# Latent query and key norms computed in the Fourier stage, and one Fourier stage for tokens and context

## The reference

```python
def rms_norm(x, g):
    xf = x.astype(jnp.float32)
    y = xf * lax.rsqrt(jnp.mean(jnp.square(xf), axis=-1, keepdims=True) + NORM_EPS) * g
    return y.astype(x.dtype)

def fourier_mix(z):
    zg = z.reshape(b, n, FNET_GROUPS, FNET_GROUP_DIM).astype(jnp.float32)   # 4 groups of 128
    return jnp.fft.fft2(zg, axes=(1, 3), norm='ortho').real                 # tokens and channels

def mixer(h, hc, lp, rope, n_rows, need_ctx):       # need_ctx: in the first layer only
    f, nq, nk, nv, cq, ckv, kr, g = jnp.split(h @ lp['w_in'], IN_OFFSETS, axis=-1)
    y_f = fourier_mix(f)
    y_na = neighbourhood_attention(...)
    mla_k, mla_v = mla_keys_values(ckv, kr, ...)    # rms_norm(ckv, g_kv) @ w_uk, @ w_uv; rope on kr
    mla_q = mla_queries(cq, ...)                    # rms_norm(cq, g_q) @ w_uq, @ w_qr; rope
    y_mla = blocked_attend(mla_q, ...)
    out = merge_branches([y_f, y_na, y_mla], g, lp['w_branch'], lp['w_out'])
    if need_ctx: the same three branches for the context
```

## Time and profile before

| | |
|---|---|
| time, median of 3 runs | 3474.93 us (3470.12, 3474.93, 3482.54) |
| the profiled execution: its time | 3475.75 us |
| its span (first to last instruction) | 3473.8 us |
| TensorE busy | 3015.1 us (87%) |
| VectorE busy | 1763.6 us (51%) |
| ScalarE busy | 1197.6 us (34%) |
| GpSimd busy | 448.9 us (13%) |
| mean granted clock of TensorE | 0.921 of 2.4 GHz |

### The profile page before, as it was taken

The page is one execution under the profiler, slowest core; times in us unless marked ns, Lnnn a source line. Parts: engine busy times, 40 slices in busy tenths (PEclk is TensorE's granted clock), DMA queues, the critical chain, the costliest instruction groups (busy, mean ns, idle before and its releaser), DMA issues. The chain is left out here.

```text
span 3473.8 us, 37971 instructions
## 1 busy us (share of the span) xinstructions
PE 3015.1 (87%) x15109; PEld 2392.6 (69%) x15109; DVE 1763.6 (51%) x2555; ACT 1197.6 (34%) x1746; POOL 448.9 (13%) x419
## 2 busy tenths in 40 slices
PE   5788879799987999999698798987999968875995
PEld 3677646688875888888487455775878745553774
DVE  4564666222236554553512763345555453644886
ACT  4322645212114211221323543223322233533884
POOL 3410310000011000001320200001000013212232
PEclk8799989999997999999899899998999988986997
DMA  5663010222212443431340102322655415514972
GB/s 158 114 161 97 1 22 1 73 55 55 55 43 67 120 122 96 118 108 51 52 94 26 22 0 73 91 73 61 182 164 173 134 28 70 162 49 150 339 269 73
DMA packets 398087, 330.33 MB, mean 95 GB/s; under 512 B 38059, under 2 KB 340697, under 8 KB 397785
## 3 DMA queue, kind: packets, MB, share of 16 engines
q1 hardware_dynamic: 384664, 304.79, 30.9%
q0 software_dynamic: 13248, 23.13, 3.4%
HBM read 332.09 MB, written 30.33 MB: 104 GB/s over the span
## 5 line engine op out<-in xcount | busy, mean ns | idle before, releaser
L1043 PE MATMUL ps<-ahi,w_hi 128*128 128x512 f32 (+1 forms) x2384 | 865.0, 363 | 164.8 <-DVE alo L710 91.5
L1045 PE MATMUL ps<-alo,w_hi 128*128 128x512 f32 (+1 forms) x2384 | 854.1, 358 | 0.0
L1044 PE MATMUL ps<-ahi,w_lo 128*128 128x512 f32 (+1 forms) x2384 | 853.5, 358 | 0.0
L1043 PEld LDWEIGHTS ps<-ahi,w_hi 128*128 128x128 f32 x2384 | 459.0, 193 | 250.6 <-issue 67.9
L1065 DVE TENSOR_TENSOR w_lo<-w_raw,w_hi 128x1024 fp32r<-128x1024 f32 (+2 forms) x248 | 359.7, 1452 | 422.9 <-ACT w_hi L1055 422.3
L1045 PEld LDWEIGHTS ps<-alo,w_hi 128*128 128x128 f32 x2384 | 458.7, 192 | 67.6
L1044 PEld LDWEIGHTS ps<-ahi,w_lo 128*128 128x128 f32 x2384 | 459.6, 193 | 63.7
L1055 ACT CAST w_hi<-w_raw 128x1024 fp32r<-128x1024 f32 (+2 forms) x248 | 289.8, 1170 | 425.8 <-PE ps L1045 349.8
L877 DVE SCALAR_TENSOR_TENSOR vec_acc<-vec_w,csilu,vec_acc 128x512 f32<-128x512 f32 x364 | 260.8, 762 | 19.9 <-DMA vec_w<-in_w_mod 15.1
L1043 PE MATMUL ps<-hhi,w_hi 128*128 128x512 f32 (+1 forms) x528 | 190.5, 361 | 10.1 <-DVE hlo L1174 10.1
L1141 POOL TENSOR_TENSOR xsum<-x 128x768 f32<-128x768 f32 (+1 forms) x4 | 7.2, 1800 | 1480.0 <-DVE x L1126 1480.0
(11 more groups left out here) (497 smaller groups left out, 5195.6 us busy)
## 6 DMA issues: line engine op xcount, KB each, us to landing
vec_w<-in_w_mod SPq DMA_DIRECT2D x128, 512.0 KB, 3.9
w_raw<-in_w_in SPq DMA_DIRECT2D x104, 512.0 KB, 4.2
e_raw<-in_w_gate SPq DMA_DIRECT2D x46, 512.0 KB
e_raw<-in_w_up SPq DMA_DIRECT2D x46, 512.0 KB
e_raw<-in_w_down SPq DMA_DIRECT2D x46, 512.0 KB
w_raw<-in_w_ffn_gate SPq DMA_DIRECT2D x44, 512.0 KB, 3.9
w_raw<-in_w_ffn_up SPq DMA_DIRECT2D x44, 512.0 KB, 3.9
w_raw<-in_w_ffn_down SPq DMA_DIRECT2D x32, 704.0 KB, 4.8
```

The lines of the kernel that those rows point to most:

```text
L1043: pe.matmul(o, whi[:, j, b0 + b, :], hi[:, b, t0:t0 + tn], start=(b == 0), stop=False)
L1044: pe.matmul(o, wlo[:, j, b0 + b, :], hi[:, b, t0:t0 + tn], start=False, stop=False)
L1045: m = pe.matmul(o, whi[:, j, b0 + b, :], lo[:, b, t0:t0 + tn], start=False, stop=(b == nb - 1))
```

## The change

Three things change, all in the first two layers.

- `fourier` takes a list of parts. In the first layer one block transforms the latent tokens (groups 0 to 3) and the context (groups 4 to 7), with one load of `dft_chan` and all loads of `dft_seq` at its start. In the second layer there is one part, as before.
- The norms of `ckv` and `cq` move out of the preparation block into this block, as class `LatentNorms`. On TensorE, ScalarE and VectorE they stand ahead of the Fourier work. Their sums use banks 6 and 7 (`ckv`) and 4 and 5 (`cq`), so `tokens(0)` waits until VectorE has read the latter. The squares have tiles of their own (`latent_sq`) where they had borrowed tiles of `proj`.
- The preparation block keeps the rope channels, the values and the loads. Its matmuls of values no longer wait for a norm.

```diff
-        def fourier(proj, t0, T, seq, chan):
+        def fourier(proj, parts, chan, latent):
...
                 def _(sp):
                     sp.dma_start(dch[:], chan).then_inc(ld[0].sem, 16)
...
+                    for part, (_, T, seq) in enumerate(parts):
+                        of_parity = seq.rearrange("(m p e) s n -> e m p s n", p=P, e=2)
+                        per = T // P // 2
+                        for n in range(T // P):
+                            sp.dma_start(dseq[part][:, n], of_parity[n // per, n % per, :, :, 0:T // 2]).then_inc(ld[1 + part].sem, 16)
...
+                    def tokens(g):
...
+                        pe.wait_ge(act_chain.sem, act_chain.base + g + 1)
+                        if g % 4 == 0:
+                            pe.wait_ge(ld[1 + g // 4].sem, ld[1 + g // 4].base + 16 * (T // P))
+                        if g >= 2:
+                            pe.wait_ge(dve_chain.sem, dve_chain.base + g - 1)
...
+                    latent.pe(pe)
                     pe.wait_ge(ld[0].sem, ld[0].base + 16)
                     channels(0)
-                    pe.wait_ge(ld[1].sem, ld[1].base + 16 * nt)
-                    for gr in range(4):
-                        if gr < 3:
-                            channels(gr + 1)
-                        tokens(gr)
+                    pe.wait_ge(norm_rstd.sem, latent.rstd0 + 2)
+                    for g in range(n_groups):
+                        if g + 1 < n_groups:
+                            channels(g + 1)
+                        tokens(g)
...
                 def _(act):
...
+                    latent.act(act)
+                    for g in range(n_groups + 1):
...
                 def _(dve):
...
+                    latent.dve(dve)
+                    for g in range(n_groups):
...
+        class LatentNorms:
...
+            def pe(self, pe):
+                for n, k in ((0, 0), (1, 1), (1, 2)):
+                    pe.wait_ge(norm_sq.sem, self.sq0 + k + 1)
+                    for t0, tn in groups(ALL if n == 0 else self.T):
+                        m = pe.matmul(self.sums[n][:, t0:t0 + tn], ones[:], self.sq[k][:, t0:t0 + tn], start=(k < 2), stop=(k != 1), skip_group_check=True)
+                    if k != 1:
+                        m.then_inc(norm_var.sem, 1)
+
+            def act(self, act):
+                for k in range(3):
+                    act.activation(self.sq[k], self.src[k], ACT.Square).then_inc(norm_sq.sem, 1)
+                for n in range(2):
+                    act.wait_ge(norm_rstd.sem, self.rstd0 + n + 1)
+                    act.activation(self.rstd[n], self.rstd[n], ACT.Sqrt).then_inc(norm_sqrt.sem, 1)
+
+            def dve(self, dve):
+                for n in range(2):
+                    dve.wait_ge(norm_var.sem, self.var0 + n + 1)
+                    dve.tensor_scalar(self.rstd[n], self.sums[n], 1.0 / (P, 2 * P)[n], LN_EPS, ALU.mult, ALU.add).then_inc(norm_rstd.sem, 1)
+                for n, parts in enumerate(((0,), (1, 2))):
+                    dve.wait_ge(norm_sqrt.sem, self.sqrt0 + n + 1)
+                    dve.reciprocal(self.rstd[n], self.rstd[n]).then_inc(norm_g.sem, 1)
+                    dve.wait_ge(norm_g.sem, self.inv0 + n + 1)
+                    for k in parts:
+                        gain = V3_QN + 2 * self.l + k - 1 if n else V3_KVN + self.l
+                        dve.scalar_tensor_tensor(out=self.src[k], in0=self.src[k], scalar=col(vec3, gain), in1=self.rstd[n], op0=ALU.mult, op1=ALU.mult)
...
                     def _(pe):
-                        pe.wait_ge(norm_sq.sem, norm_sq.base + 1)
-                        for t0, tn in groups(ALL):
-                            m = pe.matmul(sums[0][:, t0:t0 + tn], ones[:], sq[0][:, t0:t0 + tn], start=True, stop=True)
-                        m.then_inc(norm_var.sem, 1)
...
                         pe.wait_ge(ld[2].sem, ld[2].base + 16)
-                        pe.wait_ge(norm_x.sem, norm_x.base + 1)
...
                     def _(act):
-                        for n in range(3):
-                            act.activation(sq[n], src[n], ACT.Square).then_inc(norm_sq.sem, 1)
                         act.copy(eye[:], ident[:])
-                        for n in range(2):
-                            act.wait_ge(norm_rstd.sem, norm_rstd.base + 1 + n)
-                            act.activation(rstd[n], rstd[n], ACT.Sqrt).then_inc(norm_sqrt.sem, 1)
...
-                        ch.link(dve.reciprocal(rstd[0], rstd[0]))
-                        dve.scalar_tensor_tensor(out=src[0], in0=src[0], scalar=col(gain, V3_KVN + l), in1=rstd[0], op0=ALU.mult, op1=ALU.mult).then_inc(norm_x.sem, 1)
...
-                    fourier(proj, 0, LAT, g["k_dft_lat"], g["k_dft_chan"])
-                    if not last:
-                        fourier(proj, LAT, CTX, g["k_dft_ctx"], g["k_dft_chan"])
+                    sequences = [(0, LAT, g["k_dft_lat"])] + ([] if last else [(LAT, CTX, g["k_dft_ctx"])])
+                    fourier(proj, sequences, g["k_dft_chan"], LatentNorms(proj, l, T))
```

More of the change, by code:

```diff
@@ L1276, in tokens @@
                                 for s in range(2):
-                                    m = pe.matmul(ps[:, o:o + T // 2], u[:, gr, n, s * P:(s + 1) * P], dseq[:, n, s, :],
-                                                  start=(n == odd * per and s == 0), stop=(n == (odd + 1) * per - 1 and s == 1))
-                        m.then_inc(norm_var.sem, 1)
+                                    m = pe.matmul(ps[:, o:o + T // 2], u[:, g % 4, n, s * P:(s + 1) * P], dseq[g // 4][:, n, s, :],
+                                                  start=(n == parity * per and s == 0), stop=(n == (parity + 1) * per - 1 and s == 1))
@@ new lines, in fourier, with __init__, prepare, ended @@
+            for t in (pe_chain, act_chain, dve_chain, norm_x, norm_hi):
+                t.base += n_groups
+            ld[0].base += 16
+            for part, (_, T, _) in enumerate(parts):
+                ld[1 + part].base += 16 * (T // P)
+            latent.ended()
+        class LatentNorms:
+            def __init__(self, proj, l, T):
+                self.proj, self.l, self.T = proj, l, T
+                self.src = [proj[:, T_CKV, :]] + [proj[:, T_CQ + n, 0:T] for n in range(2)]
+                self.sq0, self.var0, self.rstd0, self.sqrt0, self.inv0 = norm_sq.base, norm_var.base, norm_rstd.base, norm_sqrt.base, norm_g.base
+                self.sums = [ps[:, 6 * BANK:6 * BANK + ALL], ps[:, 4 * BANK:4 * BANK + T]]
+            def prepare(self, c):
+                self.sq = [sb(c, f"latent_sq{n}", [P, t])[:] for n, t in enumerate((ALL, self.T, self.T))]
+                self.rstd = self.sq[0:2]
+            def pe(self, pe):
[22 more added lines that the diff above has]
+                        dve.scalar_tensor_tensor(out=self.src[k], in0=self.src[k], scalar=col(vec3, gain), in1=self.rstd[n], op0=ALU.mult, op1=ALU.mult)
+            def ended(self):
+                norm_sq.base += 3
+                for t in (norm_var, norm_rstd, norm_sqrt, norm_g):
+                    t.base += 2
@@ L1995, in latent_attention @@
             with ExitStack() as c:
-                gain = vec3
                 T = ALL if with_ctx else LAT
@@ L2105, in _ @@
                         dve.tensor_tensor(k32[R0:R1, 0:LAT], ra[R0:R1, :], rb[R0:R1, :], ALU.add).then_inc(prep_dve.sem, 1)
-                        dve.wait_ge(norm_sqrt.sem, norm_sqrt.base + 2)
-                        ch.link(dve.reciprocal(rstd[1], rstd[1]))
-                        for k in range(2):
-                            dve.scalar_tensor_tensor(out=src[1 + k], in0=src[1 + k], scalar=col(gain, V3_QN + 2 * l + k), in1=rstd[1], op0=ALU.mult, op1=ALU.mult)
                         dve.tensor_scalar(rope[R0:R2, :], rope[R0:R2, :], MLA_SCALE, None, ALU.mult)
```

99 lines of the change are left out of this document (42 added, 57 removed).

## The result

The changed kernel takes **3442.78 us** (median of 4 runs, 3439.48 to 3446.32), the kernel before 3473.56 (4 runs, 3470.12 to 3482.54). The ratio is 0.9912, 95% interval 0.9896 to 0.9928: faster by 0.9%. The profiled execution took 3444.96 us, 30.8 less than the profiled one of before.

What follows compares the result with a forecast made beforehand. Each stage's longest chain was taken to bound the kernel, VectorE's in the preparation blocks. Gains of 19.6 (preparation), 2.9 and 1.5 us (Fourier) sum to 24.0, taken from 3475.75: 3451.7, put as 3451 us, range 3443 to 3460.

Steps and rivals of the forecast that it cites:

- preparation 2: Second layer's preparation block: 15.2 us long instead of 25.09, 9.8 us less.
- preparation 1: First layer's preparation block: 15.2 us long instead of 25.07, 9.8 us less.
- landing: Start of each preparation block: the spread table must land before the spread matmuls, 2.2 us with 0.1 to begin.
- spread: TensorE's spread matmuls in each preparation block: 2.0 us, between 1.55 at full clock and 3.1 at the lower level.
- Fourier 1: First layer's Fourier part, two stages merged and norms added: next stage starts at 354.9 instead of 357.78, 2.9 us less.
- stall at `tokens(2)`: First layer's Fourier stage: TensorE's third latent group waits 0.8 us for VectorE, whose queue now holds the norms.
- Fourier 2: Second layer's Fourier stage: the norms' sums fit in TensorE's wait for the token table; 1.5 us less, bounds 0 and 2.
- The two `mla_klo` one after the other: End of each preparation block: GpSimd's and VectorE's halves, released together, run serially, 3.43 + 1.74 = 5.17 us.
- The two `mla_klo` overlap: Rival, preparation blocks: both halves run at once and the spread at full clock, 4.4 us more gain, 3447; chance 0.17.
- The norms are not hidden: Rival, Fourier stages: both end 3 us later than before instead of earlier, gain 13.6 us, 3462; chance 0.10.
- Another late thing in the preparation block: Rival: late weights or ScalarE's copies end the block, half of its gain stays out, 3461; chance 0.08.
- The clock, slower: Rival: TensorE stays at 1.2 GHz into the neighbourhood attention, some 70 us longer in the first layer, 3521; chance 0.03.

Runs made afterwards that it cites:

- run by turns: Changed kernel with a semaphore that lets GpSimd's `mla_klo` start only after VectorE's; 3450.72 us, a single run.
- run on VectorE alone: Changed kernel with both halves of `mla_klo` on VectorE, one after the other, and none on GpSimd; 3443.34 us, a single run.
- second profile of before: The kernel before once more, with no edit; 3470.19 us (20 runs), the profiled run 3468.42 us.
- doubled reciprocal: Changed kernel with each reciprocal of the norms computed a second time into a tile nobody reads; 3470.85 us (10 runs), ratio 0.999 to before.

## Why the prediction was nearly right, and where it failed

**The four stages.** The sum said 24.0 us, and the four stages lose 24.8 between the two profiled executions. That it came so near is luck in part: preparation 2 was 1.9 us worse than said, the Fourier stages 1.65 and 0.9 better. Term by term:

| term | predicted | measured |
|---|---|---|
| preparation 1 | 15.2 us long | 15.18 |
| of it: landing, spread, rotation, `mla_khi`, the two `mla_klo`, drain | 2.2, 2.0, 2.6, 2.9, 5.2, 0.3 | 1.80, 2.65, 2.59, 2.77, 5.04, 0.33 |
| preparation 2 | 15.2 | 17.13 (3.44, 2.96, 2.58, 2.78, 5.04, 0.33) |
| Fourier 1 | 2.9 less | 4.55 less |
| of it: stall at `tokens(2)` | 0.8 | 0.75 |
| Fourier 2 | 1.5 less | 2.41 less |

*Preparation 1* was right to 0.02 us, and that too is luck: the landing came 0.4 us sooner than said and the spread took 0.65 longer, at a granted 0.58. In the other two profiles of the changed kernel the block is 14.79 and 14.68 us.

*The two `mla_klo` one after the other* was right, in the order for which no row of before stood: VectorE issued 0.12 us earlier, and GpSimd's end came 3.28 us after VectorE's (448.11 and 444.83). Before, it was VectorE that stood behind GpSimd. The run by turns and the run on VectorE alone settle it. This is the rule in the Trainium skill, "SBUF — State Buffer", "Who interferes with whom", by which the first to issue holds the pair and the other blocks; the trace agrees in both orders, with 4.91 us for GpSimd's half that otherwise takes 3.43, and 4.16 for VectorE's two multiplies that otherwise take 1.42.

*Preparation 2* was mis-sized by 1.9 us in the terms landing (2.2, measured 3.44) and spread (2.0, measured 2.96). I priced a landing by one row of the first layer, and the spread nearer to the full clock than to the lower one; it was granted 0.50 throughout. In the changed kernel the same load took 1.80 us in the first layer and 3.44 in the second, and in the three profiles of the changed kernel the second block is 2.0 to 2.2 us longer than the first. In the run with `mla_klo` on VectorE the table landed within 1.7 us in the second layer, and there the rope table came late in its place. Why it lands late stays open.

*Fourier 1* was better than said by 1.65 us, since `tokens(0)` came 10.13 us after the start and not 11.6. The clock rose 3.7 us after the first work and not 5.6, which is worth half of the 1.9 us between; 0.35 more is in the two `channels`, which took 3.45 us (the 328.0 of the prediction holds two of 1.9, though it names one). What I took for a property of the stage was a property of one execution, as the second profile of before shows (3.6). *Fourier 2* gained 0.9 more than said; but 1.9 of its gain is there in the second profile of before as well (27.02 against 28.90), and in one profile of the changed kernel it is 28.19. Over all pairs of a profile of before with one of the changed kernel its gain lies between −1.2 and +2.4 us. And it isn't owed to sums that fit in a wait: without them the new stage takes 25.29, so they cost 1.2.

**Where it failed.** The step is the last one, "the bounds of the terms give gains from 18 … to 31, and the runs shown lie up to 8 us from their median. The range is 3443 to 3460". The sum was subtracted from one execution of 3475.75 us, and the range was given the bounds of the terms and hardly anything for the base: 3475.75 − 31 is 3444.75, so its lower end, 3443, left 1.75 us for a scatter that the same sentence puts at up to 8. (The bound of 18 is 18.9 by the terms it names, and 17.4 with nothing from the second Fourier stage.) From 3451.75 to the 3442.78 measured there are 9.0 us: 0.8 are the four stages, 5.8 are stages whose code the change doesn't touch (the rest, 3353.3 and 3347.5), 0.2 lie outside the span, and by the last 2.2 the median of the changed kernel's runs is below its profiled execution. Of the 5.8 the stretch ahead of the first Fourier stage has 1.6, the first neighbourhood stage 1.0 and all that follows the second preparation 6.1; between the first preparation and the second Fourier stage 2.9 are lost again. So the missing term is the base's, but for the 1.0: the prediction asked whether the neighbourhood stage could lose its clock, and put at nothing that it could gain, from 0.96 to 1.00. How large it had to be is seen in what came later: medians of before of 3470.19, 3474.41 and 3472.18 us over 48 runs, single ones from 3461.0 to 3486.04, and a rest between 3339.6 and 3361.7 in the twelve profiles. Whether the change itself gives more than its four stages is open: the medians differ by 26.1 to 30.8 us, the four stages of the changed kernel by 20.1 to 25.5 from those of before and the first neighbourhood stage by 0.7 to 1.0, and the intervals of the ratios reach down to 21.5.

**The rivals.** *The two `mla_klo` overlap*: refuted. *The norms are not hidden*: in the first layer they were covered but for the 3.7 us that merging pays for, in the second but for 1.2, and the margin at `tokens(2)` was below zero as said; the doubled reciprocal shows what this rival would have done from there on. *Another late thing in the preparation block*: not in the first layer; in the second the late table and the slower spread kept back 1.9 of the 9.9 us. *The clock, slower*: refuted, 1.00 granted in the neighbourhood stage after the change.

## What to carry to other kernels

Move work from a stage where its engine sets the end to one where that engine idles, and count the idle time up to the first thing that others wait for, not the whole stage: here VectorE was free until the additions that `tokens(2)` needs, the norms used that up to 0.75 us beyond it, and another 9.9 us of work there made the stage 11.7 us longer. When two engines share the end of a block, ask whether they can work at once; a helper that holds the other up is worth nothing if the stronger engine does both parts in the helper's time. And give the range of a predicted time the scatter of the base, taken from several runs, beside the bounds of the terms.

## What the runs showed of the hardware

- The duration of a GpSimd row can hold a wait: 4.91 us for an operation that takes 3.41 when VectorE is idle and 3.43 beside a reciprocal of VectorE, with nothing in the brackets to tell it. The earlier 4.16 us on VectorE was the same thing from the other side, and so were the 3.09 us of its two multiplies in the first layer (at 459.94), which take 1.95 in the changed kernel.
- The delay from TensorE's first work to the higher clock differed between executions of one program, about 5.7 and 3.6 us in the kernel before. Most of the 1.6 us between the two measurements of a stage of 40 us is that.
- Untouched code varies more than the terms of such a sum: the experts' part of the third layer, the same code in all kernels, took 331.9 to 343.2 us in the twelve profiles (336.1 and 331.9 in the two of before), and single times of before spread over 23 us in 20 runs. An effect of 25 us is plain in the stages long before it is in single times.
